# A hybrid transformer on one core: the second block's mixers with another order of steps, another place for a gain, and a transposed copy split between two engines

## The reference

```python
def second_block(x, ...):
    for l in range(2):
        xn = rms_norm(h, norm_mix[l])
        (hq, hf, hi, hg, nq, kc, vc, ksl, vsl, ksw, vsw, ngate) = split(xn @ w_in[l])
        o_hg = hgrn2_mixer(hq, hf, hi, hg, lb[l], hg_gnorm[l])
        o_nsa = nsa_mixer(nq, kc, vc, ksl, vsl, ksw, vsw, ngate, ...)
        h = h + concat([o_hg, o_nsa]) @ w_out[l]
        h = h + swiglu(rms_norm(h, norm_ffn[l]))
```

## Time and profile before

| | us |
|---|---|
| median of three runs | 3529.35 |
| the profiled execution, its own time | 3529.31 |
| its span, first to last instruction | 3527.4 |
| PE busy (share) | 3376.7 (96%) |
| DVE busy | 1558.7 (44%) |
| ACT busy | 1183.1 (34%) |
| POOL busy | 146.1 (4%) |
| DMA, share of 16 engines | 25.7% |

### The profile page before, as it was taken

The page is one execution under the profiler, slowest core; times in us unless marked ns, Lnnn a source line. Parts: engine busy times, 40 slices in busy tenths (PEclk is TensorE's granted clock), DMA queues, the critical chain, the costliest instruction groups (busy, mean ns, idle before and its releaser), DMA issues. The chain is left out here.

```text
span 3527.4 us, 44381 instructions
## 1 busy us (share of the span) xinstructions
PE 3376.7 (96%) x18486; PEld 2745.9 (78%) x18486; DVE 1558.7 (44%) x2335; ACT 1183.1 (34%) x1994; POOL 146.1 (4%) x174
## 2 busy tenths in 40 slices
PE   8999999999999999988999988999999988999999
PEld 7888765788888888857888866778888776788887
DVE  3332545543325333466333375654332466553332
ACT  3221334332222222263222244453222344443221
POOL 0000001100000000021000000000000000000000
PEclk9999999999999999999999999999999999999999
DMA  4333111232332333211333221112233221123332
GB/s 167 97 100 109 64 42 36 78 96 96 102 108 85 99 98 109 85 43 44 101 99 99 90 91 60 55 49 90 96 96 111 96 76 55 37 78 98 100 101 72
DMA packets 87638, 300.37 MB, mean 85 GB/s; under 512 B 9360, under 2 KB 14608, under 8 KB 87440
## 3 DMA queue, kind: packets, MB, share of 16 engines
q1 hardware_dynamic: 87440, 297.54, 25.7%
HBM read 295.41 MB, written 2.10 MB: 84 GB/s over the span
## 5 line engine op out<-in xcount | busy, mean ns | idle before, releaser
L234 PE MATMUL ps<-xh,whi 128*128 128x512 f32 (+1 forms) x2808 | 1073.5, 382 | 28.9 <-DMA res<-in_tab 12.1
L236 PE MATMUL ps<-xh,wlo 128*128 128x512 f32 (+1 forms) x2808 | 1050.6, 374 | 0.0
L235 PE MATMUL ps<-xl,whi 128*128 128x512 f32 (+1 forms) x2808 | 1050.4, 374 | 0.0
L215 DVE TENSOR_TENSOR wlo<-raw,whi 128x1024 fp32r<-128x1024 f32 x535 | 651.2, 1240 | 664.5 <-ACT whi L207 664.2
L207 ACT ACTIVATE whi<-raw 128x1024 fp32r<-128x1024 f32 x535 | 548.1, 1050 | 517.7 <-PE ps L357 490.9
L234 PEld LDWEIGHTS ps<-xh,whi 128*128 128x128 f32 x2808 | 532.3, 190 | 150.2 <-issue 31.8
L235 PEld LDWEIGHTS ps<-xl,whi 128*128 128x128 f32 x2808 | 532.5, 190 | 95.1 <-issue 4.6
L236 PEld LDWEIGHTS ps<-xh,wlo 128*128 128x128 f32 x2808 | 532.3, 190 | 94.4
L701 DVE TENSOR_TENSOR tmp<-tmp,ps 128x512 f32<-128x512 f32 x132 | 90.8, 688 | 808.3 <-ACT tmp L686 741.8
L356 PE MATMUL ps<-wlo,hh 128*128 128x512 f32 x1056 | 415.7, 394 | 0.0
L355 PE MATMUL ps<-whi,hh 128*128 128x512 f32 x1056 | 415.1, 393 | 0.0
(11 more groups left out here) (308 smaller groups left out, 3102.1 us busy)
## 6 DMA issues: line engine op xcount, KB each, us to landing
raw<-in_w SPq DMA_DIRECT2D x535, 512.0 KB, 3.3
rows<-in_row SPq DMA_DIRECT2D x15, 512.0 KB, 4.5
xr<-in_xt SPq DMA_DIRECT2D x2, 1024.0 KB, 7.5
xr<-in_x SPq DMA_DIRECT2D x1, 2048.0 KB, 8.0
out<-tmp SPq DMA_DIRECT2D x4, 256.0 KB, 3.3
out<-rows SPq DMA_DIRECT2D x4, 256.0 KB, 2.3
ntb<-in_tab SPq DMA_DIRECT2D x2, 320.0 KB, 4.6
nga<-in_gain SPq DMA_DIRECT2D x2, 256.0 KB, 2.6
```

The costliest lines, as they stand in the source:

```text
L215: v.tensor_tensor(self.wlo[u % NW][:, :], self.raw[u % NRAW][:, :], f32(self.whi[u % NW][:, :]), SUB).then_inc(*self.up("wlo", u))
L234: t.matmul(out, wh, xh, start=first, stop=False)
L235: t.matmul(out, wh, xl, start=False, stop=False)
L236: return t.matmul(out, wl, xh, start=False, stop=last)
```

## The change

It has five parts, all in `Nsa`.

1. `H0` is moved ahead of `cv` and `gt` (and its product from bank 4 to bank 5; the weight stream is laid out to match), `ca(1)` goes from chunk 30 to chunk 34 and `cmp(1)` from 34 to 40. The operand `xx` lives in the second half of `rows` instead of in a decay buffer, and POOL's first `rs` waits for `cmp(1)`'s end on DVE ("nxx" 1) instead of `ca(0)`.
2. `T(m)`: ACT copies bank 2 only, DVE copies bank 3. There is one buffer `pt` instead of two, so both copies wait for PV(m-1). PV(m) waits for both.
3. In a chunk `PV(m-1)` (with `o` and `xa`) now stands ahead of `T(m)` (with `rs`).
4. The gain of the recurrence's norm was a column, applied in `store` (a scale of ACT's cast, one operand of DVE's subtraction). Now it is a tile `hgn` of 128 x 128 that one more DMA brings in; `hr` multiplies each head by its inverse norm and the gain (four operations of 128 x 128 a head) right behind the reciprocal, and `hy` is one multiplication of 128 x 512 by the gate, where it was four of 128 x 128.
5. Places: `hr(0,3)` from chunk 95 to 92, `hy(0)` and `hy(1)` from 96 and 97 to 95, `hr(3,4)` from behind the stores 0 to 3 to chunk 100, ahead of the gate's eviction; `cp(0)` from 66 to 65, `ct(2)` 74 to 73, `cs(3)` 83 to 85, `h2(1)` one chunk earlier.

```diff
-    slots = "KV ck Q cv gt H0 hq0 hf0 HIa hq1 hf1 H1 hq2 hf2 HIb hq3 hf3 HGa HGb".split()
+    slots = "KV ck Q H0 cv gt hq0 hf0 HIa hq1 hf1 H1 hq2 hf2 HIb hq3 hf3 HGa HGb".split()
...
-    compressed_at = ((45, 47, 66), (60, 67, 69), (71, 74, 77), (83, 87, 91))
+    compressed_at = ((45, 47, 65), (60, 67, 69), (71, 73, 77), (85, 87, 91))
...
-        put(end("cv") + 5, ("ca", 1))
-        put(end("H0") + 1, ("cmp", 1))
+        put(34, ("ca", 1))
+        put(40, ("cmp", 1))
...
-        put(95, ("hr", 0, 3))
-        put(96, ("hy", 0))
-        put(97, ("hy", 1))
+        put(92, ("hr", 0, 3))
+        put(100, ("hr", 3, 4))
+        put(95, ("hy", 0), ("hy", 1))
...
-            put(s + 2 * m + 2, ("T", m), turn=1)
-            put(s + 2 * m + 4, ("PV", m), turn=2)
+            put(s + 2 * m + 2, ("T", m), turn=2)
+            put(s + 2 * m + 4, ("PV", m), turn=1)
...
# scalar
-                if m >= 2:
-                    a.wait_ge(*at("nPV", l, m - 2))
-                for g in range(2):
-                    a.wait_ge(*at("nT", l, m, g))
-                    a.activation(self.pt[m % 2][:, g, 0:w], c.bank(2 + g)[:, 0:w], COPY).then_inc(*up("npt", l, m, g))
+                a.wait_ge(*at("nT", l, m, 0))
+                if m:
+                    a.wait_ge(*at("nPV", l, m - 1))
+                a.activation(self.pt[:, 0, 0:w], c.bank(2)[:, 0:w], COPY).then_inc(*up("npt0", l, m))
# vector
+            elif kind == "T":
+                v.wait_ge(*at("nT", l, m, 1))
+                if m:
+                    v.wait_ge(*at("nPV", l, m - 1))
+                v.tensor_copy(self.pt[:, 1, 0:w], c.bank(3)[:, 0:w]).then_inc(*up("npt1", l, m))
...
# vector, "hr"
+                for h in range(lo, hi):
+                    v.wait_ge(*at("nvo", l, h))
+                    for i in range(4):
+                        ins = v.scalar_tensor_tensor(out=o, in0=o, scalar=self.ss[:, 4 * h + i:4 * h + i + 1], in1=self.hgain[:, :], ...)
# gpsimd, "rs"
-                g.wait_ge(*(at("nrt", l, n - 1) if n else at("nxa", l, 0)))
+                g.wait_ge(*(at("nrt", l, n - 1) if n else at("nxx", l, 1)))
```

More of the change, by code:

```diff
@@ L1347, in __init__ @@
         self.cc = c.rows[:, 0, :].rearrange("p (a t) -> p a t", t=T)
-        self.xx = self.decay[1][:, 0:992].rearrange("p (a n) -> p a n", n=62)
+        self.xx = c.rows[:, 1, 0:992].rearrange("p (a n) -> p a n", n=62)
         self.unit, self.first, u, chunk = {}, {}, u0, 0
@@ L1393, in use @@
         if kind == "T":
-            return [(2 + g, x("pt", *a, g)) for g in range(2)]
+            return [(2, x("pt0", *a)), (3, x("pt1", *a))]
         if kind == "rt":
@@ L1423, in order @@
         put(end("H1") + 1, ("h1", 1))
-        put(end("H1") + 3, ("h2", 1))
+        put(end("H1") + 2, ("h2", 1))
         put(end("gt") + 2, ("turn",))
@@ L1443, in order @@
                 put(s + 2 * m + 3, ("rt", n), turn=0)
-                put(s + 2 * m + 4, ("o", n), turn=2)
+                put(s + 2 * m + 4, ("o", n), turn=1)
                 if n % 2:
-                    put(s + 2 * m + 4, ("xa", n // 2), turn=2)
+                    put(s + 2 * m + 4, ("xa", n // 2), turn=1)
         for x, (a, b, d) in enumerate(self.compressed_at):
@@ L1459, in order @@
         out += [step for k in sorted(place) for _, step in sorted(place[k], key=lambda x: x[0])] + [("hz", 0), ("hz", 1)]
-        out += [("evac", self.slot["HGb"])] + [("store", k) for k in range(4)] + [("ahead",), ("hr", 3, 4), ("hy", 2), ("hy", 3)]
+        out += [("evac", self.slot["HGb"])] + [("store", k) for k in range(4)] + [("ahead",), ("hy", 2), ("hy", 3)]
         return out + [("store", k) for k in range(4, KD)]
@@ L1470, in tables @@
         s.dma_start(self.htb[:, :], c.tabs("near")).then_inc(*c.up("nhtb", l, by=16))
+        s.dma_start(self.hgain[:, :], c.gain[l, :, 512:640]).then_inc(*c.up("nhtb", l, by=16))
         s.dma_start(self.tb[:, :], c.tabs("seen", "cone")).then_inc(*c.up("ntb", l, by=16))
@@ L1650, in tensor @@
                 _, br, i, _ = self.score(m)
[L1651 removed]
+                t.wait_ge(*at("npt0", l, m))
+                t.wait_ge(*at("npt1", l, m))
                 for j in range(i + 1):
@@ L2367, in stream @@
             some = lambda *cols: wide(w[:, np.concatenate(cols)])
-            parts += [some(k0, k1, v0, v1), some(ck), some(2048 + order), some(cv), columns(w, gate), first[0], some(q[0]), some(f[0]),
+            parts += [some(k0, k1, v0, v1), some(ck), some(2048 + order), first[0], some(cv), columns(w, gate), some(q[0]), some(f[0]),
                       some(i[0], i[1]), some(q[1]), some(f[1]), first[1], some(q[2]), some(f[2]), some(i[2], i[3]), some(q[3]), some(f[3]),
```

43 lines of the change are left out of this document (19 added, 24 removed).

## The result

The changed kernel takes 3618.28 us (median of 4 runs, 3616.69 to 3621.68) against 3531.72 before: ratio 1.0246, 95% interval 1.0228 to 1.0264, 87 us slower. The prediction had 50 us, and the measured time lies above its range: the direction was right, the size was not.

What follows compares the result with a forecast made beforehand. TensorE (PE) was taken to set the time, its waits mostly ended by DVE or ACT. The terms summed to 25.2 us per stage, 50 for both, on 3529.31: forecast 3579.5 us, range 3547 to 3605.

Steps and rivals of the forecast that it cites:

- rt(0): After S(4): POOL's spread waits for cmp(1), now queued behind S(4)'s mask, maximum and exponentials; +2.8 us a stage.
- clock: PE at half clock behind waits at S(2), S(4) with rt(0), S(7), level 7 and the end; +2 us a stage.
- the rest: 0: One more 64 KB DMA, the buffer of xx and store's simpler forms lie under other work: 0.
- S(7): Scores S(7): DVE is in the compressed softmax until 2914.70, then copies for 0.56; S(7) comes 1.5 us later.
- with DVE at 59% I keep three quarters: Copies split, PV first: waits let DVE catch up, so the 10.6 us sum is cut to +8 a stage.
- The terms for late copies: S(m+1) waits for DVE's copy of T(m): 5.9, 3.0 and 6.5 us; S(3) with S(4) priced separately at 1.9.
- ct(1)'s credit: cp(0)'s earlier place removes ct(1)'s 2.34 us wait, a late copy of T(17) gives 1 back: -1.3 us.
- S(2): S(2) stands behind ca(1)'s eight additions and the copy of T(1)'s bank 3 on DVE; +2.6 us a stage.
- S(31): hr(0,3) at chunk 92 delays level 6's update and the bank copy on DVE; S(31) comes 5.0 us later.
- the output projection: hr(3,4) ahead of the SiLU makes its casts and first matmul 2.3 us later a stage.
- worse: Rival: late copies put DVE behind for good, clock halves at each wait; 34 us a stage, 3598; chance 0.08.
- a drain at each table load: By the page's 1380 ns price, 4 us a stage more at hr's two places, 3587; chance 0.01, within 0.08.

Runs made afterwards that it cites:

- PV first: Kernel before with only PV(m-1) put ahead of T(m), ACT still copying both halves into two buffers: 3540.8 us against 3531.2.
- the split alone: Kernel before with only T(m)'s copy split between ACT (bank 2) and DVE (bank 3), two buffers and the old order kept: 3557.7 us against 3531.2.
- the four places: Kernel before with only h2(1) at chunk 63, cp(0) at 65, ct(2) at 73 and cs(3) at 85: 3553.1 us against 3531.2.
- the first part: Kernel before with H0 ahead of cv, ca(1) at 34, cmp(1) at 40 and POOL's first spread waiting for cmp(1): 3541.7 us against 3531.1.
- hr's group: Kernel before with the gain applied by DVE in hr, hr(0,3) at 92, hy(0), hy(1) at 95, hr(3,4) ahead of the gate's SiLU: 3550.0 us against 3531.1.
- H0 early: Kernel before with only H0 ahead of cv, ca(1) at chunk 30 and cmp(1) at 34: 3534.0 us against 3531.1.
- waits filled: Changed kernel with products by a zero matrix put on PE into five of its waits per stage: 3605.8 us against 3533.6 for the kernel before.
- ca(1) and cmp(1) back: Changed kernel with ca(1) back at chunk 30 and cmp(1) at 34, H0 still early: 3609.5 us against 3533.1 for the kernel before.

## Why the prediction was wrong

The four parts, each put on the kernel before by itself, add up: 10.0 + 37.2 + 20.0 + 11.9 = 79.1 us of the 82.5 in the stages, and by the medians 89.9 of 86.6. So to within some 4 us no part worked only through another, and the prediction can be judged part by part (both stages, us; idle and busy PE add up to the stages):

| part | predicted | stages, alone | idle PE | busy PE | medians |
|---|---|---|---|---|---|
| H0, ca(1), cmp(1), rt(0) | 9.8 | 10.0 | 6.9 | 3.2 | 10.6 |
| copies, PV first (with S(3), S(4)) | 19.8 | 37.2 | 23.3 | 13.9 | 38.6 |
| h2(1), cp(0), ct(2), cs(3) | 0 | 20.0 | 11.4 | 8.6 | 21.8 |
| hr, hy, gain | 16.8 | 11.9 | 12.1 | -0.2 | 18.9 |
| clock | 4 | in the above | | | |
| sum | 50.4 | 79.1 | 53.7 | 25.5 | 89.9 |

**The step that failed most is the clock**: "I add 2 us; bounds -1 and +5" a stage. PE is busy 13.6 and 16.3 us longer, against 4 for both. That this is the clock, the other kernels bear out: with the split alone PE is busy 10.8 us longer for 23.9 more at half clock, with the four places 8.6 for 20.5, with the first part 3.2 for 13.6, with hr's group -0.2 for 3.4 (PV first has some 4 us beside it). I had the row for it, 6.9 us at 0.51 behind a wait of 2.8 us, and counted five waits of that size; but I priced them at 2 us together, while filling such a wait gave back 1.1 to 2.6 us. The second stage has eleven stretches at half clock after, three before. I had also read the second stage alone, with 13.7 us at half clock; the first has 20.4 behind its first matmul, for the same list, and would have asked for a wider bound.

**Second, "the rest: 0"**: the moved places of the compressed attention were in the diff, and the order showed them, but I credited `cp(0)` with removing ct(1)'s wait of 2.34 us and did not ask what it waits for itself; h2(1), ct(2) and `cs(3)` have no term at all. ct(1)'s wait and cp(0)'s are of one kind: a product that uses bank 7 waits for ACT to copy out what the bank held, and that copy stands in ACT's list behind the attention's exponentials. Before, this was cp(0)'s result ahead of ct(1); moved into the chunk of rt(3), cp(0) itself waits for rt(3)'s (1.7 us), ct(2) for rt(4)'s (2.15) and h2(1) for h1(1)'s (1.6). cs(3) is the case of S(7), which stood in the rows: a compressed softmax one chunk ahead of a T(m) holds its copy, and S(7) waits 2.32 us. Before, cs(3) stood one chunk ahead of T(25), and S(26) started without a wait: PE had `val(2)` to do meanwhile. Between T(26) and S(27) it has nothing.

**Not a failed step** is "with DVE at 59% I keep three quarters". The terms for late copies, 17.3 us a stage, met 16.7 more wait at S; less the 2.9 that T saves this would be 13.8 of idle time, and 11.7 are there, since the waits inside the levels shrank by 1.9. Without ct(1)'s credit, which belongs to another part, the prediction has 11.9 x 3/4 + 1.9 = 10.8. That is near, though the argument for the factor, DVE's mean busy share, was not tested. The price of DVE's copy was right as well (0.28, 0.42, 0.55 and 0.69 us by width; 0.38 to 0.69 and a mean of 0.5 predicted). What this part costs beyond the forecast is its 13.9 us of busy PE, which is the first step again.

Right were: DVE as the engine that sets PE's waits; S(2) (+2.6 predicted, 2.5; but with ca(1) moved back it is no less, so the number is right and the cause only in part), S(3) and S(4) (1.9; 2.6), S(7) (1.5; 1.3), S(9) (1.1; 1.1), S(13) (1.9; 1.7); S(14) half as large (1.4; 0.7); rt(0) (2.8; 3.9 with the clock behind it); S(31) (5.0; 4.9); the output projection (2.3 behind a late T(31); 1.8). The idle time as a whole was 23.2 a stage against 26.3, which is partly luck: the places, at 0, were too low by 5.7 and hr's 8.4 too high by 2.4.

Of the rivals, "worse" (34 a stage, 3598) was the nearest, with a chance of 0.08, and still too low: it took 5 us for the clock. The other part of that case, a drain at each table load, is not there. ACT in the kernel after, ahead of level 7's products:

```profile
3162.38 1.28 ACT L1804 ACT_TABLE_LOAD   x1
...
3163.67 0.30 ACT L1804 ACTIVATE hss<-hss,vc 128x12 f32<-128x12 f32 x1
```

The load takes 1.28 us, the price that the Trainium skill gives ("ScalarE: Activation LUTs", What ACT_TABLE_LOAD costs), and the square root starts 0.01 us behind it; the 1380 ns drain of that page does not show in this trace.

## What to carry to other kernels

Where the bounding engine waits often and briefly, price the clock with the waits: here slower matmuls took more than half as much as new idle time (30.7 us against 52.7). Look for each moved step at what it waits for itself, not only at what it no longer blocks: here four moved steps cost 20 us. And expect a part of many small waits to be given back by others that shrink: here about 2 of 14 us a stage, which is far from all of them, though DVE was idle 41% of the stretch.

## What the runs showed of the hardware

The same wait does not always bring the clock down. S(4) waits 2.82 us in each of these two kernels; in the first (H0 early) the following 6.9 us run at 1.00, in the second (H0, ca(1), cmp(1)) the clock falls 1.2 us after S(4) starts and stays at 0.50 for 10.2 us.

```profile
2896.45 0.49 PE L1638 MATMUL ps<-nk,nq 64*128 64x128 f32 x4 [2.82 <-ACT rows L1821]
...
2896.40:2903.30 6.90, 5.59 (x51) 4.88 (x51) 2.44 (x6) 2.91 (x9) 0.61 (x1) 1.00 0.19 59
```

```profile
2898.26 0.49 PE L1638 MATMUL ps<-nk,nq 64*128 64x128 f32 x4 [2.82 <-ACT rows L1821]
...
2899.50:2909.70 10.20, 6.03 (x27) 5.04 (x25) 2.50 (x3) 3.49 (x8) 1.47 (x1) 0.50 0.15 51
```

In the kernel before it was 6.9 us. In the same way two edits that lie elsewhere (waits filled; ca(1) and cmp(1) back) brought half clock, and 3.1 us, to S(16) and S(17) in both stages. So it takes the sum of many places to see what the clock costs. What decides between the cases, the runs don't settle.
